# Experts of a two-layer mixture-of-experts block: routing matrix per pair of experts, eight weight slots, and loads moved between stages

## The reference, cut to what matters

```python
# x (1, 512, 1024); 16 experts, capacity 64, inner width 1024
h = rms_norm(x, g_mix[i])                       # opens the layer; h @ w_in[i] follows
...                                             # branches, among them attention with a relative bias
def expert_choice_moe(h, w_router, w_gate_e, w_up_e, w_down_e):
    affinity = softmax(h @ w_router, axis=-1)                    # (1, 512, 16)
    top_aff, idx = top_k(swapaxes(affinity, 1, 2), 64)           # 64 tokens per expert
    xe = h[bidx, idx]
    hid = silu(einsum('becd,edf->becf', xe, w_gate_e)) * einsum('becd,edf->becf', xe, w_up_e)
    ye = einsum('becf,efd->becd', hid, w_down_e)
    return zeros_like(h).at[bidx, idx].add(ye * top_aff[..., None])
x = x + expert_choice_moe(rms_norm(x, g_moe[i]), ...)
x = x + sigmoid(rms_norm(x, g_ple[i]) @ w_ple_gate[i]) * (p[i] @ w_ple[i])
```

## Time and profile before

| | |
|---|---|
| profiled execution | 4260.53 us, its span 4258.8 us |
| granted TensorE clock, mean | 0.934 of 2.4 GHz |
| TensorE busy | 3643.9 us (86%) |
| VectorE busy | 1711.8 us (40%) |
| ScalarE busy | 1048.9 us (25%) |
| bytes read from HBM, mean rate | 640.00 MB, 154 GB/s over the span |
| expert stages | from 714.61 to 1212.5 us and from about 2001 to 2500.6 us |

### The profile page before, as it was taken

The page is one execution under the profiler, slowest core; times in us unless marked ns, Lnnn a source line. Parts: engine busy times, 40 slices in busy tenths (PEclk is TensorE's granted clock), DMA queues, the critical chain, the costliest instruction groups (busy, mean ns, idle before and its releaser), DMA issues. The chain is left out here.

```text
span 4258.8 us, 45164 instructions
## 1 busy us (share of the span) xinstructions
PE 3643.9 (86%) x17408; PEld 2415.4 (57%) x17408; DVE 1711.8 (40%) x2996; ACT 1048.9 (25%) x1623; POOL 24.6 (1%) x34
## 2 busy tenths in 40 slices
PE   7669996999987769986999885998899969998998
PEld 5546674434445646665444443765666746666666
DVE  2475643111132475743111133236744322476433
ACT  2233321000022233321000022333332124333321
POOL 0010000000000010000000000000000000000000
PEclk9879997999998879997999997999999989999999
DMA  4021124999943121123999954111122241111222
GB/s 150 28 87 51 62 87 185 408 416 408 409 162 113 37 87 50 54 91 151 410 413 408 409 200 178 60 40 45 55 80 75 89 189 50 48 47 56 74 75 99
DMA packets 133511, 653.03 MB, mean 153 GB/s; under 512 B 20836, under 2 KB 43364, under 8 KB 67032
## 3 DMA queue, kind: packets, MB, share of 16 engines
q1 hardware_dynamic: 128088, 642.17, 39.1%
q10 hardware_dynamic: 5248, 8.52, 0.6%
HBM read 640.00 MB, written 14.84 MB: 154 GB/s over the span
## 5 line engine op out<-in xcount | busy, mean ns | idle before, releaser
L1430 PE MATMUL ps<-normed_T_hi,ring_split 128*128 128x512 f32 (+1 forms) x1952 | 639.1, 409 | 40.9 <-PEq L268 14.6
L1430 PEld LDWEIGHTS ps<-normed_T_hi,ring_split 128*128 128x128 f32 (+1 forms) x1952 | 370.5, 193 | 154.6 <-issue 44.8
L1430 PE MATMUL ps<-normed_T_lo,ring_split 128*128 128x512 f32 (+1 forms) x976 | 388.8, 398 | 0.0
L2079 PE MATMUL ps<-normed_T_hi,ring_split 128*128 128x512 f32 x1024 | 339.4, 413 | 18.5 <-DVE branches L2338 16.5
L1706 DVE TENSOR_TENSOR ring_split<-weight_ring,ring_split 128x2048 fp32r<-128x2048 f32 x76 | 174.0, 2290 | 301.4 <-ACT ring_split L1591 301.3
L1027 PE MATMUL ps<-weight_ring,projected 128*64 128x512 f32 x1280 | 281.0, 593 | 15.4 <-DVE projected L1072 15.4
L2079 PEld LDWEIGHTS ps<-normed_T_hi,ring_split 128*128 128x128 f32 x1024 | 194.9, 194 | 90.6 <-issue 29.7
L257 PE MATMUL ps<-weights_hi,normed_T_hi 128*128 128x472 f32 (+1 forms) x512 | 199.4, 389 | 44.8 <-DVE weights_lo L369 34.5
L1430 PEld LDWEIGHTS ps<-normed_T_lo,ring_split 128*128 128x128 f32 (+1 forms) x976 | 187.5, 192 | 42.5
L1090 DVE TENSOR_TENSOR residual<-residual,ps 128x512 f32<-128x512 f32 x128 | 88.0, 688 | 290.9 <-PE ps L1048 290.9
L2079 PE MATMUL ps<-normed_T_lo,ring_split 128*128 128x512 f32 x512 | 204.0, 398 | 0.0
(11 more groups left out here) (391 smaller groups left out, 5792.2 us busy)
## 6 DMA issues: line engine op xcount, KB each, us to landing
weight_ring<-in_w_exp_gate SPq DMA_DIRECT2D x96, 1024.0 KB, 18.9
weight_ring<-in_w_slabs SPq DMA_DIRECT2D x78, 1024.0 KB, 4.9
spare_weights<-in_w_exp_up SPq DMA_DIRECT2D x64, 1024.0 KB, 24.6
weight_ring<-in_w_exp_up SPq DMA_DIRECT2D x64, 1024.0 KB, 11.1
spare_weights<-in_w_exp_down SPq DMA_DIRECT2D x64, 1024.0 KB, 17.1
weight_ring<-in_w_branch_gate SPq DMA_DIRECT2D x32, 1024.0 KB, 5.0
weight_ring<-in_w_exp_down SPq DMA_DIRECT2D x32, 1024.0 KB, 13.4
weight_ring<-in_w_ada SPq DMA_DIRECT2D x16, 1536.0 KB, 12.7
```

Source lines behind the costliest of these rows:

```text
L1430: ins = e.matmul(dst, lhs(k, m), rhs(k, m), start=k == 0 and m == 0, stop=k == KD - 1 and m == 2)
L2079: ins = e.matmul(dst, lhs(k, m), rhs(k, m), start=k == 0 and m == 0, stop=k == KD - 1 and m == 2)
```

## The change

- `chosen` is built for one pair at a time (`choose`, 512 elements a partition), the first in the route stage, the next ones during the pair before. `weigh` multiplies it by the affinities; TensorE turns the product in four transposes, ScalarE copies it to `spread`. The DRAM table goes, with its writes and reads.
- The gather of the next pair stands between the down products and the spread of this one. TensorE waits for the adds bank by bank ahead of the gate and up products, where before all eight adds were awaited. The loops of TensorE and SP take two pairs a turn; TensorE's last two pairs stand behind the loop.
- Eight weight slots in place of six. The router's weights and six slots are loaded by SP in the norm stage before, the other two in the route stage once the router's products have read the normed input, in whose place they lie.
- The bias is spread by SP at the end of the projection stage.
- p, half of w_ple and of w_ple_gate are loaded by SP at the end of the expert stage; ScalarE splits the gate weights ahead of its takes.

```diff
@@ norm_stage, SP
-                    if ple is not None:
-                        e.dma_start(p_T, a["p"][ple, :, :, :]).then_inc(s["side_landed"], 16)
-                        e.dma_start(ple_side[:, :, :], ple_side_w(ple, 0)).then_inc(s["side_landed"], 16)
-                        for kh in range(2):
-                            land(e, s, kh, a["w_ple_gate"][ple, kh * 512:(kh + 1) * 512, 0:512], 512)
...
                     for dst, src in loads:
                         e.dma_start(dst, src).then_inc(s["inputs_loaded"], 16)
+                    if experts_of is not None:
+                        for v in range(6):
+                            load_expert_weights(e, experts_of, 0, v)
                     if loads:
                         e.wait_ge(s["inputs_loaded"], 16 * len(loads))
-                    if spread_bias:
-                        for h in range(4):
-                            e.dma_start(skew[h:h + 1, :]...[:, 0:1024], bias_rows[h, :].partition_broadcast(P)).then_inc(s["side_landed"], 16)
-                        e.wait_ge(s["side_landed"], 64)
@@ project_stage, SP, after its last load: the four lines of spread_bias
@@ norm_stage, ScalarE, ahead of scaled_hi (it stood behind)
+                    if ple is not None:
+                        e.wait_ge(slot_loaded[0], EXPERT_LOADS + 16)
+                        e.activation(W_hi[:, 0, :], landing[:, 0, :], ACT.Copy).then_inc(s["slab_hi"], 1)
@@
-        halves = [W[:, ...] for n in range(6)] + [T[:, 4096:6144], Zr[:, 9216:11264]] + [spare[:, ...] for n in range(4)]
+        halves = [W[:, ...] for n in range(6)] + [R[:, ...] for n in range(3)]
+        halves += [Zr[:, ...] for n in range(2, 5)] + [spare[:, ...] for n in range(4)]
+        def choose(e, i):
+            return e.tensor_tensor(chosen..., iota..., ranks_tok[:, :, bass.ds(i * 2, 2)]..., ALU.is_equal)
+        def weigh(e, i):
+            return e.tensor_tensor(weighted..., chosen..., affinity[:, :, bass.ds(i * 2, 2)]..., ALU.mult)
@@ route_stage
-                    e.dma_start(wr, a["w_router"][l, :, :]...).then_inc(s["inputs_loaded"], 16)
-                    for v in range(4):
-                        load_expert_weights(e, l, 0, v)
-                    e.wait_ge(s["stage_a"], 1)
-                    for v in range(4, 6):
+                    e.wait_ge(s["product_ready"], 1)
+                    for v in range(6, 8):
                         load_expert_weights(e, l, 0, v)
...
-                    for t in range(NT):
-                        e.tensor_tensor(chosen[:, t, :]..., ALU.is_equal).then_inc(...)
+                    choose(e, 0).then_inc(s["vector_step"], st.add("vector_step"))
@@ expert_stage, SP
+                    for u in range(8, 24):
+                        e.wait_ge(s["weights_free"], u - 7)
+                        load_expert_weights(e, l, 0, u)
+                    with e.Fori(1, n_pairs // 2) as i2:
+                        for u in range(24):
+                            e.wait_ge(s["weights_free"], i2 * 24 + (u - 7))
+                            load_expert_weights(e, l, i2, u)
+                    for kh in range(2):
+                        e.wait_ge(s["weights_free"], 12 * n_pairs - (7 - kh))
+                        e.dma_start(landing[:, kh, :]..., a["w_ple_gate"]...).then_inc(slot_loaded[kh], 16)
+                    e.wait_ge(s["weights_free"], 12 * n_pairs - 5)
+                    e.dma_start(p_T, a["p"][l, :, :, :]).then_inc(slot_loaded[2], 16)
+                    e.dma_start(ple_side[:, :, :], ple_side_w(l, 0)).then_inc(slot_loaded[2], 16)
@@ expert_stage, TensorE, pair i
+                        e.wait_ge(s["pool_ready"], i + 1)
+                        for t in range(NT):
+                            ins = e.transpose(PS[:, 4, t * P:(t + 1) * P], weighted[:, t, :], ident)
+                        ins.then_inc(s["rotated"], 1)
                         e.wait_ge(s["stage_b"], i * 2 + 2)
-                        e.wait_ge(s["stage_h"], i * 8 + 8)
                         for v in range(8):
+                            if v % 2 == 0:
+                                e.wait_ge(s["stage_h"], i * 8 + (5 + v // 2))
                             products(v)
...
                         for v in range(8, 12):
                             products(v)
+                        if not last:
+                            e.wait_ge(s["hi_ready"], i + 1)
+                            gather(i + 1)
                         e.wait_ge(s["output_taken"], i + 1)
-                        e.wait_ge(s["output_ready"], i + 1)
                         for q in range(8):
...
@@ expert_stage, ScalarE: the four reads of route go; ahead of the sigmoid
+                        e.wait_ge(s["rotated"], i + 1)
+                        e.activation(spread, PS[:, 4, :], ACT.Copy).then_inc(s["output_ready"], 1)
@@ expert_stage, VectorE, pair i
+                        if not last:
+                            e.wait_ge(s["pool_ready"], i + 1)
+                            choose(e, i + 1).then_inc(s["hi_ready"], 1)
                         e.wait_ge(s["stage_c"], i + 1)
...
                         e.tensor_copy(hid_T[:, 512:1024], PS[:, 7, :]).then_inc(s["stage_g"], 1)
+                        if not last:
+                            e.wait_ge(s["hi_ready"], i + 1)
+                            e.wait_ge(s["rotated"], i + 1)
+                            weigh(e, i + 1).then_inc(s["pool_ready"], 1)
+                            take_gathered(i + 1)
                         for q in range(8):
```

More of the change, by code:

```diff
@@ L44 @@
 N_EXP, CAP, FF = 16, 64, 1024
+EXPERT_LOADS = 32 * 12 * (N_EXP // 2) // 8
 MAXH = 8
@@ new lines, in mixer_kernel @@
+        ranks_tok = small[:, 256:320].rearrange("p (t n) -> p t n", t=NT)
+        router_w = T[:, 4096:4224].rearrange("p (k n) -> p k n", k=KD)
+        halves = [W[:, 2048 * n:2048 * (n + 1)] for n in range(6)] + [R[:, 2048 * n:2048 * (n + 1)] for n in range(3)]
+        halves += [Zr[:, 2048 * n:2048 * (n + 1)] for n in range(2, 5)] + [spare[:, 2048 * n:2048 * (n + 1)] for n in range(4)]
+        ring = [[halves[2 * n + ex].rearrange("p (k n) -> p k n", k=4) for ex in range(2)] for n in range(8)]
@@ L987, in expert_stage @@
             s = signals.stage()
[L988 to L992 removed]
+            xe = Zr[:, 10240:11264].rearrange("p (k n) -> p k n", k=KD)
+            sig, hid, hid_T = (T[:, 1024 * i:1024 * i + 1024] for i in range(3))
             hid_Tv = hid_T.rearrange("p (k n) -> p k n", k=KD)
+            sig2, hid2 = (v.rearrange("p (b n) -> p b n", b=2) for v in (sig, hid))
+            n_pairs = N_EXP // 2
             with nc.Block() as block:
@@ L1047, in _ @@
                                 e.wait_ge(s["stage_h"], i * 8 + (q + 5))
-                            e.matmul(PS[:, q % 4, :], spread[:, t * P:(t + 1) * P], ye[:, half * 512:(half + 1) * 512], start=True, stop=True).then_inc(s["side_ready"], 1)
+                            e.matmul(PS[:, q % 4, :], spread[:, t * P:(t + 1) * P], result[:, half, :], start=True, stop=True).then_inc(s["side_ready"], 1)
+                    e.sem_inc(s["stage_h"], 8)
+                    gather(0)
+                    with e.Fori(0, n_pairs // 2 - 1) as i2:
+                        pair(i2, 0, False)
+                        pair(i2, 1, False)
+                    pair(n_pairs // 2 - 1, 0, False)
+                    pair(n_pairs // 2 - 1, 1, True)
                 @block.scalar
                 def _(e):
-                    e.sem_inc(s["pool_ready"], 1)
-                    with e.Fori(0, N_EXP // 2) as i:
-                        e.wait_ge(s["pool_ready"], i + 1)
-                        for ex in range(2):
-                            for dst, which in ((who, 0), (weight, 1)):
-                                src = route[which, bass.ds(i * 2 + ex, 1), :].to_broadcast([64, S])
-                                e.dma_start(dst[ex * 64:(ex + 1) * 64, :], src).then_inc(s["inputs_loaded"], 16)
+                    with e.Fori(0, n_pairs) as i:
+                        e.wait_ge(s["rotated"], i + 1)
+                        e.activation(spread, PS[:, 4, :], ACT.Copy).then_inc(s["output_ready"], 1)
                         e.wait_ge(s["weights_free"], i * 12 + 4)
-                        e.activation(sig.rearrange("p (b n) -> p b n", b=2), PS[:, 0:2, :], ACT.Sigmoid).then_inc(s["stage_c"], 1)
+                        e.activation(sig2, PS[:, 0:2, :], ACT.Sigmoid).then_inc(s["stage_c"], 1)
                         e.wait_ge(s["stage_e"], i * 2 + 1)
```

103 lines of the change are left out of this document (44 added, 59 removed).

## The result

The changed kernel took 4197.0 us, the median of four executions (4189.99 to 4202.15), against 4260.97 of the kernel before in the same session: a ratio of 0.985, 95% interval 0.983 to 0.987. The prediction had 4182 us in a range of 4170 to 4203. The executions of the kernel before lie within 2 us of each other, those of the changed one within 12.

A forecast was written before the change was run, and what follows sets the result against it. TensorE's order was taken as the chain in the expert stages, the weight stream almost as long. Gains 29.8 + 7.2 + 14.4 + 11.4 + 15.4 = 78.2 us off 4260.5 gave 4182 us, range 4170 to 4203.

The forecast's parts named there:

- A: Expert stages: the weight stream binds after all, still needing 62.5 us a pair; time 4199, chance 15%.
- B: Route, first norm and embedding: something stays covered by another wait, half of 41.2 us; time 4203, chance 8%.
- Inside the experts: Expert stages: gather moved between down products and spread removes TensorE waits; pair becomes 59.1 us, gain 29.8 us in all.
- The experts' term: First gather to last add, both layers: new order 29.8 us plus late pairs' DMA waits 7.2, together 37.0 us.
- The stream: Expert weight loads: eight slots' store covers the deficit, so the stream follows; late pairs' waits go too, 7.2 us together.
- Route, 14.4: Route stage: router's weights loaded earlier, 3.2 us a layer, and smaller 0/1 matrix, 4.0 us a layer; sum 14.4 us.
- First norm, 11.4: First norm of each layer: without the bias spread the save starts earlier; gains 4.8 and 6.6 us, sum 11.4.
- Embedding, 15.4: Embedding inputs: loaded earlier, p's products hidden and ScalarE's weight copy before its takes; 7.7 us a layer, sum 15.4.
- the five stretches: Execution cut from first norms to the embedding's first add; predicted gains 11.4, 6.4, 8.0, 37.0 and 15.4 us.
- C: Loop over expert pairs: longer loop code costs instruction loading at loop ends and exits, up to 30 us; time 4212, chance 4%.
- D: Expert stages: eight outstanding slots let the stream drop to 353 GB/s, a pair taking 71.3 us; time 4322, chance 2%.

The follow-up runs named there:

- again: The changed kernel run and profiled once more, unaltered: 4199.6 us, ratio 0.986.
- the filled one: Changed kernel with useless TensorE transposes, eight and six, in the two idle stretches between gate/up and down products of each pair: 4183.29 us.
- experts_only: Changed kernel with the moved loads of bias, router's weights and embedding inputs put back; experts' part, pairwise choice and eight slots stay: 4227.89 us.
- three_six: three_parts with six weight slots in place of eight: 4173.71 us, ratio 0.980.
- split_reads: Changed kernel with next pair's gather in two halves (4168.22 us), plus ScalarE's queue reading four unused broadcast rows a pair: 4200.17 us.
- three_parts: Changed kernel with next pair's gather split: four blocks ahead of the hidden transposes, two behind them, two ahead of the spread: 4156.56 us.
- six_slots: Changed kernel with six weight slots in place of eight, all else the same: 4198.99 us, ratio 0.985.

## Why the prediction was right, and which term was off

The measured 4197 us lies in the range, but 7 us outside the forecast's own part of it (4173 to 4190). The range reached that far for rivals A and B, with 4199 and 4203, and neither is what happened. So it is in part luck that the time lies in the range; the mechanism is borne out stretch by stretch, except for the two terms that come first here.

*1. Inside the experts, the mis-sized term.* "The pair becomes 59.1 us": it is 59.6. The prediction let 1.41 + 1.22 = 2.63 us of waits go. By the starts of TensorE's records in the two traces, the distance from the last down product to what follows shrinks from 1.71 to 0.52 us, and that from the last gather record from 1.23 to 0.11: 2.31 together. The four transposes take 0.53, where 0.5 was predicted. And the down products now start 31.08 us behind the pair's first product, where it was 30.93: the idle stretch ahead of them grew from 0.83 to 0.97 us, which the prediction took as unchanged. 61.24 - 2.31 + 0.53 + 0.15 = 59.61, measured 59.62. This is 0.5 us in seven pairs of two layers, 7 us.

*Beside it, the clock.* The prediction counted the granted clock as 1.00 in the expert stage and looked for gains elsewhere. It put the low stretches of the expert stages at nothing, in the kernel before and in the changed one. The profiled execution of the kernel before has three low stretches in the expert stages, the changed one four and, in "again", six, the filled one none; at 1.7 us each. The experts' term is then 37.0 - 7 - 1.7 = 28.3 in the profiled execution (measured 26.5), 37.0 - 7 - 5.1 = 24.9 in "again" (23.8) and 37.0 - 7 + 5.1 = 35.1 with the hole filled (36.0): within 2 us each time. That the filled kernel comes to 4183, where 4182 was forecast, is luck: the pair's 7 us and the falls' 5.1 us cancel for the most part.

*2. The stream.* It follows, as predicted: no wait for a DMA, no dip per pair, half the bytes change nothing. What keeps it ahead was given wrongly: at the changed kernel's pair six slots do as well, so it is the removed reads that keep the stream ahead. Their price was read from q10's share (1.6 us a pair) where the late pairs already said up to 3.

*3. Route, 14.4.* Measured 15.8, 13.1 and 12.2: the wait for the router's weights (3.0 to 3.6 a layer against 3.2) and the choice (2.8 to 5.1 against 4.0) are both on the path. The stretch from router to first gather also holds the router's own products and transposes, which meet low stretches of differing length (3.4 and 23.9 us in the first layer of the changed kernel, 6.8 and 20.5 in "again"), so its spread of 3 us need not be the choice's. SP's twelve issues took 9.8 us, predicted 10.4, and end before VectorE.

*4. First norm, 11.4.* Measured 10.1 to 13.1, over a stretch that runs through the whole mixer. Within the norm itself the projection's load goes out 4.4 and 6.3 us earlier after the stage's start, where 4.8 and 6.6 were predicted. The save goes out at 13.98 and is covered. The four bias DMAs take SP 2.54 us behind the projection's last load, and the spread's 10 us lie under its last products.

*5. Embedding, 15.4.* Measured 15.5 up to the embedding's first product, and 16.0 to 17.6 up to its first add. p's products take 7.11 us at the full pace, where the earlier trace rows had 9.58 with part of them at the lower clock; put back at their old place (experts_only) they take 8.63 us behind a wait of 7.16 for in_w_ple.

*The rivals.* A, the stream still at 62.5 us a pair without the route reads, fell: it needs 59.1 to 59.3 (three_six), and the reads were the cost (split_reads). B fell with the five stretches. C: the page counts 124 instruction packets in place of 110, and the pair is 59.6 at every turn of the loop and at its exit. D: the stream holds 422 GB/s with eight slots.

The Trainium skill, TensorE: Matmul & The Clock Gate, section Part 4: PE-mode transpose, says that transposes don't count as busy time for the clock as products do. By that rule the filled holes should have helped little, if it holds for these float32 transposes; but eight or six of them per pair took the low stretches of the expert stages from six to none, and 14 to 16 us went. The measurement decides.

## What to carry to other kernels

What a wait is worth is the distance of the two starts around it less the engine's own pace: 1.71 - 0.43 = 1.28 and 1.23 - 0.11 = 1.12 us here, of which 2.31 us came. The idle column, 1.11 and 0.96, is smaller, since the records of TensorE overlap where nothing waits (0.59 us long at a pace of 0.43). Then look at what the new order adds to the waits that stay, here 0.15 us. When an order is made denser, look at what idle time is left beside it and put the next piece of work there; here the half of a gather in the hole between two products won its own idle time and steadied the clock as well. A spread between executions of a kernel whose neighbour had none is itself a reading: compare the granted clock of its stretches before looking for a late transfer. It is a sign and no proof: three_parts spreads over 6 us with no low stretch in the expert stages of its profiled execution.

## What the runs showed of the hardware that was not expected

- Two idle stretches of 1.33 and 0.97 us, 1 us of transposes between them, can lower TensorE's granted clock to 1.2 GHz for 3.4 us, and this happens in some pairs and in others not, with the same instructions: one to six of a layer's eight from run to run, 1.7 us each. With either stretch filled the profiled execution had none.
- Slow pairs come in rows of up to six (six_slots; 61.4 us from one low stretch to the next, at pairs of 61.3), and in every layer that has any the first pair is one of them. Single ones and rows of two also stand at the end of a layer. What sets off the first and ends a row was not found.
- Four reads a pair of 2 KB rows, broadcast to 64 partitions each (0.5 MB written), cost the weight stream 3.1 us of a pair (62.5 in split_reads against 59.4), the time of 1.3 MB at 424 GB/s.
